# Attention in steps of four key tiles, pipelined across heads, with loads and stores of the branches around it placed anew

## The reference: what is computed

```python
h = rms_norm(x, norm[l])
proj = h @ w_in[l]
...
qk = jax.nn.silu(causal_depthwise_conv(m_qk, conv_w[l], conv_b[l]))
...
hm = mlstm_chunkwise(mq, mk, mv, ig, lf)
...
q_all = (rms_norm(a_cq, cq_norm[l]) @ w_uq[l]).reshape(B, S, A_HEADS, A_DQK)
...
ha = causal_block_attention(qa, ka, v_a) * jax.nn.silu(a_z)
...
hc = memory_attention(...) * jax.nn.silu(c_z)
...
merged = g_m * (hm @ w_br_m[l]) + g_a * (ha @ w_br_a[l]) + g_c * (hc @ w_br_c[l])
x = x + merged @ w_out[l]
```

## Time and profile before

| | |
|---|---|
| median of 3 runs | 2751.95 us (2750.35 to 2952.0) |
| the profiled execution | 2748.97 us |
| span of its slowest core, core 1 | 2747.7 us |
| spans of all cores | 2732.5 to 2747.7 us |
| mean granted clock of PE, by core | 0.995 to 0.997 |

### The profile page before, as it was taken

One profiled execution on the slowest core, in us unless ns is written; L12 is line 12 of the kernel. 1 busy time (PEld: TensorE's weight loads), 2 busy tenths in 40 slices (PEclk: granted clock), 3 DMA queues, 4 the chain that ended last, 5 costly groups with the idle time before them and its releaser, 6 DMA issues.

```text
span 2747.7 us, 41837 instructions; the slowest of 8 cores (2732.5 to 2747.7 us)
## 1 busy us (share of the span) xinstructions
PE 2693.6 (98%) x14037; PEld 1300.4 (47%) x14037; DVE 1059.3 (39%) x1788; ACT 892.9 (32%) x1741; POOL 617.0 (22%) x924
## 2 busy tenths in 40 slices
PE   7999899999999999999999999999999999999998
PEld 3544344564446644454555444444444444444444
DVE  6645377548576556244434311111111111111433
ACT  5532356436565454254544211111111111110212
POOL 0003100100210121277760122222222222221000
PEclk9999999999999999999999999999999999999999
DMA  9657724532544324556645744445475544447562
GB/s 252 130 131 159 193 62 108 117 98 55 105 104 108 78 41 86 96 141 155 166 107 147 170 77 76 78 74 79 77 165 92 95 75 77 76 78 131 193 206 87
DMA packets 142211, 312.38 MB, mean 114 GB/s; under 512 B 14833, under 2 KB 73009, under 8 KB 134961
## 3 DMA queue, kind: packets, MB, share of 16 engines
q0 software_dynamic: 42048, 134.27, 30.6%
q1 hardware_dynamic: 95634, 162.32, 18.9%
q10 hardware_dynamic: 4320, 13.11, 1.5%
HBM read 371.22 MB, written 72.68 MB: 162 GB/s over the span
## 4 chain that ended last, share of the span: by engine, by line
PE 92%; DMA 5%; ACT 1%; DVE 1%; issue 1%; POOL 1%; SPq 0%; ACTq 0%; POOLq 0%; DVEq 0%
PE bk L290 91%; DMA xt<-x 1%; DMA xo<-x 1%; DMA QRT<-ob 1%; DMA cz<-CZ 0%; DMA HMT<-hm 0%; PE bk L514 0%; SPq L135 0%; DMA QNT<-ob 0%; DMA mb<-BH 0%; PE bk L535 0%; PE bk L1188 0%; PE bk L1234 0%; DVE ro L303 0%; PE bk L1338 0%
## 5 line engine op out<-in xcount | busy, mean ns | idle before, releaser
L290 PE MATMUL bk<-hT,wg 128*128 128x512 bf16 x3072 | 682.3, 380 | 0.0
L290 PE MATMUL bk<-w,hT 128*128 128x512 bf16 (+1 forms) x3072 | 598.3, 345 | 7.5 <-DMA w<-wA 2.9
L290 PE MATMUL bk<-hT,w 128*128 128x512 bf16 x2112 | 489.6, 380 | 0.0
L290 PEld LDWEIGHTS bk<-hT,wg 128*128 128x128 bf16 x3072 | 300.5, 98 | 361.5 <-issue 1.6
L290 PEld LDWEIGHTS bk<-w,hT 128*128 128x128 bf16 x3072 | 296.3, 98 | 251.8 <-issue 16.2
L294 ACT ACTIVATE sh<-bk 128x512 f32<-128x512 f32 x184 | 109.8, 597 | 850.1 <-PE bk L290 850.1
L290 PE MATMUL bk<-hb,wb 128*128 128x512 bf16 x1536 | 346.7, 379 | 0.0
L290 PEld LDWEIGHTS bk<-hT,w 128*128 128x128 bf16 x2112 | 204.9, 98 | 228.8 <-issue 4.7
L310 DVE SCALAR_TENSOR_TENSOR tm<-sh,bk 128x512 f32<-128x512 f32 x124 | 85.3, 688 | 559.2 <-PE bk L290 559.2
L290 PEld LDWEIGHTS bk<-hb,wb 128*128 128x128 bf16 x1536 | 150.1, 98 | 181.1
L303 DVE TENSOR_TENSOR den<-den,Pa 128x512 f32<-128x512 f32 (+3 forms) x288 | 186.4, 647 | 103.4 <-ACT Pa L294 75.1
(11 more groups left out here) (180 smaller groups left out, 2433.1 us busy)
## 6 DMA issues: line engine op xcount, KB each, us to landing
wg<-wGB POOLq DMA_DIRECT2D x96, 512.0 KB, 5.3
w<-wA POOLq DMA_DIRECT2D x48, 516.0 KB, 9.2
wb<-wGB POOLq DMA_DIRECT2D x96, 256.0 KB, 4.1
xt<-x SPq DMA_DIRECT2D x16, 1024.0 KB, 13.3
xo<-x SPq DMA_DIRECT2D x16, 1024.0 KB, 6.8
out<-xo SPq DMA_DIRECT2D x15, 1024.0 KB, 7.4
wo<-wOUT POOLq DMA_DIRECT2D x4, 2048.0 KB, 17.5
w<-wA POOLq DMA_DIRECT2D x16, 500.0 KB, 12.2
```

What stands on the lines that cost most here:

```text
L290: fw.op("pe", lambda e: e.matmul(bk[o] if not isinstance(o, bass.AP) else o, lhsT=lhsT, rhs=rhs, start=start, stop=stop), reads=reads, wri ...
```

## The change

Attention: one step of scores now takes four key tiles (all four `kn` products, then all four `kr` products, then the masks, then four exponentials and additions), and one list of groups runs over heads, query blocks and key steps, so that a group's scores are recorded ahead of the value products of the group before, across query blocks and heads. There are 8 `Pa` tiles and 3 `den` tiles, f3 comes at the tick of f2, and the side starts at MLA with ratio 0.345. All loads of head 0 and of `kr` are now recorded after MLA. Projection: a tile `ob` is tracked in two halves, each stored when its two column blocks are there. Recurrence: it may start at V1; its sums come before it needs ML, which is now set after the second tile of `oz3`; the gates of chunk c + 1 are loaded in chunk c, behind the scores of the next chunk; ACT stores `hm`. Branch C waits 8 before the recurrence's last tail and 1 behind it (4 and 4 before). `d_gen`: `wb` is loaded one piece after each of the first four gate units; at the end the final norm's gain comes after four tiles of x and the last output weight after the third tile of x has landed.

```diff
-            ob = Ring(tiles("ob", 6, [128, S], BF16))
-
-            def part(o, c, bk, r_bk, first):
-                evac_copy(o[:, c], bk[:, 0:512], [r_bk], [o.r] if first else [], [] if first else [o.r])
+            ob = Ring(tiles("ob", 6, [128, S], BF16, n=2))
+
+            def part(o, tb, bk, r_bk):
+                evac_copy(o[:, tb * 512:(tb + 1) * 512], bk[:, 0:512], [r_bk], *half(o, tb))
+
+            def half(o, tb):
+                return ([], [o.rs[tb // 2]]) if tb % 2 else ([o.rs[tb // 2]], [])
...
-                tt("pool", o[:, cols], t1[:], t2[:], ALU.add, [t1.r, t2.r], [o.r] if tb == 0 else [], [o.r] if tb else [])
+                tt("pool", o[:, cols], t1[:], t2[:], ALU.add, [t1.r, t2.r], *half(o, tb))
...
-            marks.add("MLA0")
...
-                    for ci in (2, 0, 1):
+                    for ci in ((2, 0, 1) if pr or tb else (0, 1, 2)):
...
-                                copy("act", o[:, cols], bk[:, 0:512], [r_bk], [o.r] if tb == 0 else [], [o.r] if tb else [])
+                                copy("act", o[:, cols], bk[:, 0:512], [r_bk], *half(o, tb))
...
-                for ci in range(2):
-                    hh = 2 * pr + ci
-                    fw.dma("sp", QNT_d[hh * 128:(hh + 1) * 128, :], o3[ci][:], reads=[o3[ci].r], accs=[dr("QNT", hh)])
-                fw.dma("sp", QRT_d[pr * 128:(pr + 1) * 128, :], o3[2][:], reads=[o3[2].r], accs=[dr("QRT", pr)])
-                if pr == 0:
-                    marks.add("UQ0")
+                    if tb % 2:
+                        c = slice(tb * 512 - 512, tb * 512 + 512)
+                        for ci in range(2):
+                            hh = 2 * pr + ci
+                            fw.dma("sp", QNT_d[hh * 128:(hh + 1) * 128, c], o3[ci][:, c], reads=[o3[ci].rs[tb // 2]], accs=[dr("QNT", hh)])
+                        fw.dma("sp", QRT_d[pr * 128:(pr + 1) * 128, c], o3[2][:, c], reads=[o3[2].rs[tb // 2]], accs=[dr("QRT", pr)])
...
+                marks.add("V1")
...
                     marks.add("MG%d" % t_)
-                    if t_ == 3:
+                    if t_ == 1:
                         marks.add("ML")
...
+            yield ("need", "MLA")
             kr = mem.alloc("kr", [128, S], BF16, top=True)
...
-            vxs = tiles("vx", 1, [128, 16, 128], BF16, top=True)
+            vxs = tiles("vx", 2, [128, 16, 128], BF16, top=True)
...
-            yield ("need", "UQ0")
             loads_qk(0)
-            yield ("need", "MLA")
-            vxs += tiles("vxb", 1, [128, 16, 128], BF16, top=True)
             azs = tiles("az", 2, [128, S], BF16, top=True)
-            Ps = Ring(tiles("Pa", 4, [128, 512], BF16, top=True))
-            accs_ = Ring(tiles("den", 2, [128, 512], F32, top=True))
+            Ps = Ring(tiles("Pa", 8, [128, 512], BF16, top=True))
+            accs_ = Ring(tiles("den", 3, [128, 512], F32, top=True))
...
-                later(5, f3)
+                later(4, f3)
...
+            groups = [(h, qb, kq) for h in range(8) for qb in range(4) for kq in range(qb + 1)]
...
+            def emit_S(h, qb, kq):
...
+                if kq == 0:
+                    accd[h, qb] = accs_.next()
+                acc = accd[h, qb]
+                its = []
+                for k in range(4 * kq, 4 * kq + 4):
+                    n = (4 * qb + 4 - max(k, 4 * qb)) * 128
+                    its.append((k, n, slice(4 * qb * 128 + 512 - n, 4 * qb * 128 + 512), slice(k * 128, (k + 1) * 128), SBk.next()))
+                for k, n, qc, kc_, (bs, r_bs) in its:
+                    mm(bs, r_bs, (slice(None), slice(0, n)), kn[:, kc_], qn[:, qc], True, False, [kn.r, qn.r])
+                for k, n, qc, kc_, (bs, r_bs) in its:
+                    hf = slice(64 * (k % 2), 64 * (k % 2) + 64)
+                    mm(bs, r_bs, (slice(None), slice(0, n)), kr[hf, kc_], qr[hf, qc], False, kq < qb, [kr.r, qr.r])
+                if kq == qb:
+                    for k, n, qc, kc_, (bs, r_bs) in its:
+                        mm(bs, r_bs, (slice(None), slice(0, 128)), identb[:], mneg[:], False, True, [RC, mneg.r])
+                res = []
+                for k, n, qc, kc_, (bs, r_bs) in its:
+                    p = Ps.next()
+                    act(p[:, 0:n], bs[:, 0:n], AF.Exp, [r_bs], [p.r], scale=SC)
+                    if k == 0:
+                        copy("dve", acc[:], p[:], [p.r], [acc.r])
+                    else:
+                        o = 512 - n
+                        tt("dve", acc[:, o:512], acc[:, o:512], p[:, 0:n], ALU.add, [acc.r, p.r], [acc.r])
+                    res.append((k, p, n))
+                return res
+
+            nxt = emit_S(*groups[0])
...
+            yield 7 * MM
+            for gi, (h, qb, kq) in enumerate(groups):
+                cur_ = nxt
+                if gi + 1 < len(groups):
+                    nxt = emit_S(*groups[gi + 1])
+                    yield 6 * MM
+                if kq == 0:
                     po, r_po = POk.next()
-                    acc = accs_.next()
-                    nkt = 4 * qb + 4
-
-                    def emit_S(kt):
-                        prs = []
...
-                            k = kt + j
-                            n = (4 * qb + 4 - max(k, 4 * qb)) * 128
-                            prs.append((k, n, slice(4 * qb * 128 + 512 - n, 4 * qb * 128 + 512), slice(k * 128, (k + 1) * 128), SBk.next()))
-                        for k, n, qc, kc_, (bs, r_bs) in prs:
-                            mm(bs, r_bs, (slice(None), slice(0, n)), kn[:, kc_], qn[:, qc], True, False, [kn.r, qn.r])
...
-                        for k, n, qc, kc_, (bs, r_bs) in prs:
-                            p = Ps.next()
-                            act(p[:, 0:n], bs[:, 0:n], AF.Exp, [r_bs], [p.r], scale=SC)
...
-                    q = emit_S(0)
+                vx = vxs[h % 2]
+                for k, p, n in cur_:
+                    mm(po, r_po, (slice(None), slice(512 - n, 512)), vx[:, k, :], p[:, 0:n], k == 0, k == 4 * qb + 3, [vx.r, p.r])
                     tick()
-                    yield 3 * MM
-                    for kt in range(nkt):
-                        if kt % 2 == 0 and kt + 2 < nkt:
-                            q += emit_S(kt + 2)
-                        p, n = q.pop(0)
-                        mm(po, r_po, (slice(None), slice(512 - n, 512)), vx[:, kt, :], p[:, 0:n], kt == 0, kt == nkt - 1, [vx.r, p.r])
-                        tick()
-                        yield 2.5 * MM * n / 512
-                    finish(h, qb, acc, po, r_po)
+                    yield MM * n / 512
+                if kq == qb:
+                    finish(h, qb, accd.pop((h, qb)), po, r_po)
...
-            yield ("need", "ML")
...
+            yield 1.5
...
-            yield 1.0
+            yield 1.5
...
+            yield ("need", "ML")
...
-                loads_g(c + 2)
...
-                    fw.dma("sp", HMT_d[cp // 4, :, cp % 4, :], hm2[0][:].rearrange("p a b -> p (a b)"), reads=[hm2[0].r], accs=[dr("HMT", cp // 4)])
+                    fw.dma("act", HMT_d[cp // 4, :, cp % 4, :], hm2[0][:].rearrange("p a b -> p (a b)"), reads=[hm2[0].r], accs=[dr("HMT", cp // 4)])
...
+                if c > 0:
+                    loads_g(c + 1)
...
-            yield 4.0
+            yield 8.0
             P["mtail"]()
             hos = Ring(tiles("ho", 2, [128, 8, 128], BF16, top=True))
             Ps = Ring(tiles("Pc", 4, [128, 512], BF16, top=True))
-            yield 4.0
...
-            for _ in range(4):
-                bload()
...
+                bload()
...
-            wo_load(3, mem.alloc("wo3", [128, 16, 512], BF16))
+            wo3 = mem.alloc("wo3", [128, 16, 512], BF16)
...
-            fw.dma("sp", gfin[:], gf_d, writes=[gfin.r])
...
             for t in range(6):
                 xload(t)
+                if t == 3:
+                    fw.dma("sp", gfin[:], gf_d, writes=[gfin.r])
+            for r in cur[2].rs:
+                fw.wait_res("pool", r)
+            wo_load(3, wo3)
...
-        sides = [(mla_gen, "MLA0", 0.38), (mlstm_gen, "ML", 0.34), (c_gen, "CZ0", 0.7)]
+        sides = [(mla_gen, "MLA", 0.345), (mlstm_gen, "V1", 0.34), (c_gen, "CZ0", 0.7)]
```

More of the change, by code:

```diff
@@ L703, in part_v @@
                 evac_copy(ov[:, 4 * (u % 2):4 * (u % 2) + 4, u // 2, :], bk[:, 0:512].rearrange("p (h c) -> p h c", h=4), [r_bk],
-                          [o.r] if u == 0 else [], [o.r] if u else [])
+                          o.rs if u == 0 else [], o.rs if u else [])
             w = w_get("uk")
@@ L723, in p1_gen @@
                     t1s = Ring(tiles("ro", 4, [128, 512], F32))
-                fw.dma("sp", KNT_d[hh * 128:(hh + 1) * 128, :], o[:], reads=[o.r], accs=[dr("KNT", hh)])
+                fw.dma("sp", KNT_d[hh * 128:(hh + 1) * 128, :], o[:], reads=o.rs, accs=[dr("KNT", hh)])
             w_done("uk")
@@ L1034, in mla_gen @@
             loads_az(0)
[L1035 removed]
+            groups = [(h, qb, kq) for h in range(8) for qb in range(4) for kq in range(qb + 1)]
```

(7 more changed lines are left out.)

24 lines of the change are left out of this document (3 added, 21 removed).

## The result

The changed kernel takes 2845.28 us (median of 4 runs, 2842.74 to 2846.99) against 2751.23 for the kernel before: ratio 1.0342, 95% interval 1.0322 to 1.0362. The forecast was 2728.7, in a range of 2706 to 2745. The profiled execution has a span of 2844.3 us, 96.6 more than before.

The account below looks back on a forecast made before the run. PE was taken as the bound, busy 2693.6 of 2747.7 us. The terms summed to -23.3 against the profiled 2748.97, giving 2725.7; with 3.0 for the median, 2728.7, range 2706 to 2745.

Parts of the forecast that it names:

- rival D: Attention score groups: the `kr` halves no longer run side by side, about 27 us, time 2756; chance 0.05.
- rival B: Attention score groups: the second `kr` pair in a group pays its own switch, +8 us, time 2737; chance 0.15.
- Rival C: Attention denominators: PE waits for DVE and POOL, half of 32 waits costing 1 us, time 2743; chance 0.10.
- Score groups: Attention: groups of four halve the switches between `kn` and `kr` products, 80 times 0.20 us, -16 us.
- Denominators: Attention: less PE work covers the denominator's chain on DVE and POOL, +1.5 us (0 to 8).
- First loads: Attention start: head 0's loads land behind the next weights; PE waits 12.5 us (0 to 15), plus 2 slow, +14.5.
- Projection: Query projection: the 6.8 us of `ob` waits go, with slow clock behind and small change, -9.8 us.
- Recurrence: Recurrence: `hm` wait and slow clock go, -8.2; earlier sums, -1.0; ML two tiles sooner, +1.5 (0 to 4).
- memory attention: Memory attention and gates: spread `wb` loads remove the 2.5 us wait and 1.6 slow clock, -4.1 (0 to -4.1).
- `xo`: Program's last part: x is loaded ahead of the final norm's gain, so the 0.8 us wait goes, -0.8.
- `rdc`: End of `c_gen`: eight product pairs for six and DVE's uncovered product add +1.3 us (0 to 3).

Follow-up runs that it names:

- e9: Changed kernel with the next score group recorded between the second and third value product, not ahead of the first; ratio 1.0154 to the kernel before.
- e5: Changed kernel with each addition into `den` recorded with its value product, not four in a row behind the exponentials; ratio 1.0405 to the kernel before.
- e2: Changed kernel with the denominator's sum in the value product's own PSUM bank, not in a score bank; ratio 1.0222 to the kernel before.
- e4: Changed kernel with score steps of two key tiles instead of four, in the same list; ratio 1.0054 to the kernel before.
- e13: e10 with each addition into `den` recorded with its value product; ratio 0.9992 to the kernel before.
- e3: Changed kernel with `kr` loaded before the query projection, head 0's other loads behind the first pair's stores, `ha` single; ratio 1.0277 to the kernel before.
- e1: Changed kernel with the attention of before, its early loads and ratio 0.38, all other edits kept; ratio 0.9992 to the kernel before, some 2746 us.
- e8: Changed kernel with the denominator in the value product's bank, additions at value products, yields 1 and 2.25, early head 0 loads; ratio 1.0001 to the kernel before.
- e15: e1 with the mark ML back behind the fourth tile of `oz3`; ratio 0.9992 to the kernel before.
- e10: e9 with head 0's loads behind the second pair's stores, `kr` before the query projection, `den` two tiles; ratio 1.0091 to the kernel before.
- e17: e13 with yields 2 and 2 for score group and value product, and 6.0 for 2.5 after the recurrence's first loads; ratio 0.9899 to the kernel before.

## Why the prediction was wrong, point by point

The prediction gave a time over 2807 a chance of 0.01, and only if rival D and a new wait came together. It came without D, by waits alone: PE's idle time, forecast at about 50 us, is 137.3. The range was also added up wrongly: B, C and a wait of 15 give 2728.7 + 8 + 14.5 + 2.5 = 2753.7 as its upper end, and not 2745. The measured time lies far outside either.

- **Score groups, -16: right.** 33.3 us beyond the streams before, 17.3 after. Rivals B and D did not occur: inside a group of four the two halves start together, and the third `kr` product starts 0.23 us after the first, one stream: it does not wait as rival B had it. By the rule in "TensorEngine Tiling (Array Packing)" of the Trainium skill (Key Properties) the switch is paid per change of mode; the trace agrees with 0.22 us for two, for a group of four as for one of two.
- **Denominators, +1.5 (0 to 8): this step failed.** It measured the cover from the emission of the split to its product, and let DVE arrive after 1.7 us. In the trace of the change DVE arrives when the additions and the convolution ahead of the split let it (431.27 in the rows above), and PE waited 27.4 us for `hia` and `loa`. The cover fell by half, from about 4.7 to 2.4 us in the median of the 32 cases, as the prediction had counted; what it left out is the rest of DVE's queue, the convolution above all. e9, which makes the cover some 7 us without touching the step of four, takes both waits away. The order on DVE that I named as a reason (four additions ahead) is not borne out: e5 took them away and `hia` rose. But e5 also makes the last addition of the split's own sum late, so it does not clear the order altogether.
- **The bank: not in the sum at all.** The ring of score banks has four places and the denominator uses one of them. A step of two left it alone for a whole further step; a step of four needs all four, so its last product waits for ACT, 29.8 us in 20 waits. e2 took the wait away, with 21.2 us for `ua` in the place of it and of `hia`; e4 (two tiles) took it away as well. Nothing in the trace of before had a row for it; the code had. I counted `Pa` and `den` tiles and never the banks.
- **Additions in a row: not in the sum either.** 15.4 us for `GIF`, shown by e5 and e13 (2.9 and 3.0).
- **Rival C** had the right place for a part of it, DVE and POOL at the denominators: a price of 16 us where these two waits measure 27.4. All five are 90.0.
- **First loads, +14.5: right in kind, small in size.** 17.4 us, over the bound of 15 for the wait, and 18 in time by e3. The term that was too small is the landing of `gmh`, 26 us after the end of the projection for 22: it was issued only 1.4 us sooner after that end than before (5.8 for 7.2) and took 20.1 us for 17.3. By the rule in "DMA: Bandwidth & Descriptors" of the Trainium skill (Queues, rings and completion order) the small loads let the weights pass; the trace agrees, `gmh` landed with the last of them.
- **Projection, -9.8: right in the change** (no wait for `ob`), where no load stands between the stores. With the loads back behind the first pair 3.7 to 5.0 us return (e1, e3, e8, e15), behind the second pair none (e10).
- **Recurrence, -8.2 and -1.0; memory attention, -4.1; `xo`, -0.8: each removed wait went, the sum did not come.** In e1 these edits and the projection's, 21 us by the forecast, gave 2; the projection's wait for `ob` was 4.4 there. New waits took their place: `e` 5.1, `kw` 3.6, `ho` 2.6. The 1.3 us added for `rdc` did not come: it has 1.9 in all, for 4.1 before. For `e`, e17 shows the cause: the first `mb` load has nothing to hide it. I had priced the sums' move at a gain and not asked what the first reader of the reloaded sums would find. `kw` went in e15 and in e17; `ho` was not tried.

Sum of the failed terms, an estimate: the waits of the denominator and of `GIF` (72.6 us) for the 1.5 forecast, and the slow clock, some 29 us by PE's busy time (13.4 more although 16 went), some 21 of it between 330 and 1000 us, where these waits lie, by a granted clock of 0.94 to 0.98 there. That makes 100. The miss of 116.6 us, less 15 to 19 that the other edits fell short of and 5 of the first loads, is 93 to 97. No run parts the slow clock by wait.

## What to carry to other kernels

Before a step is made larger, count what a step holds of every ring it draws from, the PSUM banks first, and who else draws from the same ring. A step that takes the whole ring is serialised with whatever reads last. And measure the distance between an operation and its consumer in PE work around it, not in ticks of a generator: moving one call by two products took back 52 us here, and the same reordering on DVE was worth nothing before that and 27 us after it. Fixes behind one another in a chain must be tested together, since each alone only shows the next.

## What was not expected of the hardware

- Short waits were dear here. Three of 1.3 to 1.8 us within 6.0 us were followed by 6.0 us of work at a granted clock of 0.50 (755.0 to 761.0). After the one wait of 17.4 us, during which the clock had already fallen, it was 4.4 us (312.9 to 317.3). In all some 29 us of the loss came at the lower level, a third of the added idle time of 83.2.
- ACT loads a function table, 1.28 us, ahead of a denominator's logarithm; of all its table loads there were 54 before and 56 after. It cost nothing before; in the change it is more than half of the 2.4 us from the sum to the free bank.
- The loads of 128 KB and more on SP's queue issued under the four pieces of `w` landed some 20 us later, whether 128 KB (`gmh`) or 512 (`qn`), with 12.7 in the median for the first three pieces themselves.
